# Hybrid decoder layer on one core: projection products moved ahead of the value products and transposes of each attention turn

## What is computed

```python
def reference(x, ...):                       # x: (1, 1024, 1024) float32
    xn = rms_norm(x, norm_mix_w[l])
    proj = xn @ w_in[l]                      # 6 parts of 512 columns: b, c, h, q, k, v
    ...
    yc = short_conv_mixer(c_b, c_c, c_h, conv_w[l])      # b * conv3(c * h)
    qh = rms_norm(to_heads(q), q_norm_w[l]).transpose(0, 2, 1, 3)     # 8 heads of 64
    kh = rms_norm(to_heads(k), k_norm_w[l]).transpose(0, 2, 1, 3)
    ya = stick_breaking_attention(qh, kh, vh).transpose(0, 2, 1, 3)
    ...
    x = x + jnp.concatenate([yc, ya], axis=-1) @ w_out[l]
    x = x + hierarchical_moe(rms_norm(x, norm_ffn_w[l]), ...)         # 32 experts, top 2

def stick_breaking_attention(q, k, v):       # in blocks of 128 queries, keys up to the block's end
        z = jnp.einsum('bhqd,bhkd->bhqk', qb, kb) * scale
        log_keep = jnp.where(mask, jax.nn.log_sigmoid(-z), 0.0)
        ...
        suffix = lax.cumsum(shifted, axis=3, reverse=True)
        A = jnp.where(mask, jnp.exp(jax.nn.log_sigmoid(z) + suffix), 0.0)
        outs.append(jnp.einsum('bhqk,bhkd->bhqd', A, vb).astype(v.dtype))
```

## Time and profile before

| | us |
|---|---|
| median of 3 runs | 1353.81 (1353.19 to 1359.11) |
| the profiled execution, its own time | 1361.15 |
| its span in the trace | 1359.5 |
| attention stage, about 115 to 565 of the span | 450 |
| PE busy in these 450 us | 416.47 |
| experts, about 750 to 1300 of the span | 550 |

### The profile page before, as it was taken

How to read it: one execution, slowest core, us unless ns; L and a number is a source line. 1 busy time by engine, 2 the same in 40 slices (tenths; PEclk the granted TensorE clock), 3 DMA queues, 4 the chain that set the end, 5 groups by cost and what they waited for, 6 DMA issues and landing times. The chain is left out here.

```text
span 1359.5 us, 16775 instructions
## 1 busy us (share of the span) xinstructions
PE 1218.1 (90%) x5870; PEld 984.5 (72%) x5870; DVE 871.8 (64%) x910; ACT 732.6 (54%) x918; POOL 146.9 (11%) x194
## 2 busy tenths in 40 slices
PE   6999989979998998799945999999999999999930
PEld 5887767757776776588834888888888888888830
DVE  4314434445335446533264999999999999999935
ACT  5332523453354244421104788888888888888820
POOL 1000000000000003010002011111111111111000
PEclk9999969988998998899956999999999999999975
DMA  7111100100100103331064899999999999999509
GB/s 205 33 31 32 32 16 16 32 15 1 32 16 16 32 16 124 140 155 47 32 263 149 317 375 384 389 386 381 380 386 381 380 383 385 378 386 388 206 17 370
DMA packets 57339, 261.89 MB, mean 193 GB/s; under 512 B 13008, under 2 KB 33488, under 8 KB 43984
## 3 DMA queue, kind: packets, MB, share of 16 engines
q1 hardware_dynamic: 46928, 240.31, 46.4%
q0 software_dynamic: 9216, 16.80, 3.3%
q10 hardware_dynamic: 1152, 4.19, 0.8%
HBM read 252.88 MB, written 25.17 MB: 205 GB/s over the span
## 5 line engine op out<-in xcount | busy, mean ns | idle before, releaser
L1246 DVE TENSOR_TENSOR e_lo<-W,e_hi 128x1024 fp32r<-128x1024 f32 x384 | 452.6, 1220 | 25.2 <-ACT e_hi L1240 22.3
L1240 ACT ACTIVATE e_hi<-W 128x1024 fp32r<-128x1024 f32 x384 | 403.4, 1060 | 96.4 <-PE ps L1211 94.5
L731 DVE TENSOR_TENSOR_SCAN kept<-kept 128x128 f32<-128x128 f32 (+7 forms) x64 | 91.0, 1422 | 228.6 <-ACT kept L588 191.7
L1209 PE MATMUL ps<-e_hi,xT_hi 128*128 128x512 f32 x512 | 204.2, 399 | 7.1 <-DVE e_lo L1246 7.1
L1211 PE MATMUL ps<-e_lo,xT_hi 128*128 128x512 f32 x512 | 201.3, 393 | 0.0
L1210 PE MATMUL ps<-e_hi,xT_lo 128*128 128x512 f32 x512 | 200.7, 392 | 0.0
L587 ACT ACTIVATE soft<-ps,q_scale 128x128 f32<-128x128 f32 (+7 forms) x54 | 38.1, 705 | 200.4 <-PE ps L456 189.2
L407 PE MATMUL ps<-xnT_hi,w_hi 128*128 128x512 f32 x320 | 128.9, 403 | 14.4 <-DVE u L699 6.9
L407 PE MATMUL ps<-xnT_lo,w_hi 128*128 128x512 f32 x320 | 128.5, 402 | 0.0
L407 PE MATMUL ps<-xnT_hi,w_lo 128*128 128x512 f32 x320 | 128.3, 401 | 0.0
L1209 PEld LDWEIGHTS ps<-e_hi,xT_hi 128*128 128x128 f32 x512 | 97.5, 190 | 26.9 <-issue 4.0
(11 more groups left out here) (211 smaller groups left out, 1845.8 us busy)
## 6 DMA issues: line engine op xcount, KB each, us to landing
W<-in_w_dram SPq DMA_DIRECT2D x96, 2048.0 KB, 10.7
w_raw<-in_w_in_dram SPq DMA_DIRECT2D x20, 512.0 KB, 4.0
yy<-y_rows SPq DMA_DIRECT2D x8, 1024.0 KB, 13.3
xt<-in_x_dram SPq DMA_DIRECT2D x8, 512.0 KB, 3.8
w_out_raw<-in_w_out_dram SPq DMA_DIRECT2D x4, 1024.0 KB, 8.0
xn_rows<-xn SPq DMA_DIRECT2D x8, 512.0 KB, 2.6
out_dram<-x ACTq DMA_DIRECT2D x8, 512.0 KB, 8.9
x<-in_x_dram SPq DMA_DIRECT2D x1, 3072.0 KB, 13.6
```

What stands on the lines that cost most here:

```text
L731: dve.tensor_tensor_scan(back, back, back, 1.0, ALU.mult, ALU.min).then_inc(multiplied, 1)
L1209: pe.matmul(o, xs_hi[:, k], e_hi[:, p, cols], start=(k == 0), stop=False)
L1240: act.activation(e_hi[:, p], flat[:, p * D:(p + 1) * D], ACT.Copy).then_inc(s["hi_made"], 1)
L1246: dve.tensor_tensor(e_lo[:, p], flat[:, p * D:(p + 1) * D], e_hi[:, p], ALU.subtract).then_inc(s["lo_made"], 1)
```

## The change

In a turn of PE the projection products are issued directly behind `scores(n + 1)`, ahead of `values(n - 2)` and `turn(n - 1)`, except in turns `JOIN[p]`, `JOIN[p] + 1` and `JOIN[p] + 2`, which keep the old order. In every turn of ScalarE the projection banks are emptied directly behind `open_unit(n + 1)`, ahead of `take_values` and `take_turned`. VectorE, GpSimd and SyncE keep their lists. No instruction is added or taken away.

```diff
--- before.py
+++ after.py
@@ -482,11 +482,15 @@
                     p, r = divmod(n, PU)
                     if r != JOIN[p] + 1 and n + 1 < UNITS:
                         scores(n + 1)
+                    early = r not in range(JOIN[p], JOIN[p] + 3)
+                    if early:
+                        project(ticks_by(n - 1), ticks_by(n))
                     if n >= 2:
                         values(n - 2)
                     if n:
                         turn(n - 1)
-                    project(ticks_by(n - 1), ticks_by(n))
+                    if not early:
+                        project(ticks_by(n - 1), ticks_by(n))
                     if r == JOIN[p] and p + 1 < NPAIR:
                         sums_of_qk(p + 1)
                     if r == JOIN[p] + 1:
@@ -633,12 +637,13 @@
                     p, r = divmod(n, PU)
                     if r != JOIN[p] + 1 and n + 1 < UNITS:
                         open_unit(n + 1)
+                    if n:
+                        for g in groups_in(n - 1):
+                            take(g)
                     if n >= 9 and n % 8 == 1:
                         take_values(n // 8 - 1)
                     if n:
                         take_turned(n - 1)
-                        for g in groups_in(n - 1):
-                            take(g)
```

## The result

| | before | changed |
|---|---|---|
| median, us | 1356.03 (4 runs, 1353.19 to 1359.11) | 1399.88 (4 runs, 1397.87 to 1402.61) |
| profiled execution, its own time | 1361.15 | 1401.07 |
| its span | 1359.5 | 1399.4 |

The changed kernel takes 1.0327 times as long, with a 95% interval of 1.0297 to 1.0358: 40 to 49 us more, 44 by the medians. The forecast was 33 more.

A forecast was written before the change was run, and what follows sets the result against it. PE's own work was taken to bound the attention stage, so every new hole adds: 18.0 us for scores plus 15.0 for projection banks, 33 on 1353.8, gives 1387 us; own range 1378 to 1396, 8 in 10 1367 to 1408.

The forecast's parts named there:

- Both mechanisms of the sum: PE's new waits in attention: for scores' second banks, 18.0 us, and for projection banks, 15.0 us.
- What bounds the stage: Attention stage: PE's own work sets an ordinary turn, busy 416.47 of 450 us; reordering can only fill or open holes.
- Part 1: Scores directly behind transposes: the second bank waits for the previous unit's opening in 17 turns, 18.0 us together.
- the formula: Wait per scores' second bank: opening less 0.51 us, from 0.75 in two pieces to 1.61 at 1024 columns.
- Part 2: Projections brought forward lose values and transposes as cover while their bank is emptied: waits of 15.0 us beyond Part 1.
- Part 3: ScalarE empties banks first: `probsT` comes one or two copies of 0.62 us later, covered by projections; taken as 0.
- The joins: Turns 9 to 11 keep their order and VectorE still empties behind weighing: holes stay, no delay won back.
- The second rival: New holes in attention also lower PE's clock, 19 us more: 1406 us, range 1396 to 1415; chance 0.20.
- Only part 1: Banks are emptied in time, so only the scores' waits of 18 us count: 1372 us, range 1366 to 1378; chance 0.18.
- nothing: PE's true slack per turn absorbs the waits, no measurable change: 1354 to 1360 us; chance 0.07.
- faster: Earlier projections fill banks sooner and shrink two holes at the joins by 5 us: 1344 us; chance 0.05.

The follow-up runs named there:

- the third buffer: A third `soft` buffer, added to the changed kernel: 1344.61 us, 0.9915 times the kernel before; added to the kernel before: 1340.29 us, 0.9878.
- the second profile: The kernel before, profiled again unchanged: span 1352.4 us; turns 11 to 13 of pair 0 took 20.4 us, against 26.1 in its first profile.

## Why the prediction was right, and where it was off

The measured 1399.88 us lie in the range of 8 in 10 (1367 to 1408) and outside the forecast's own range (1378 to 1396). Both mechanisms of the sum were found in their places; 10 of the 43 us were not in the sum.

- **What bounds the stage.** Right. PE has no holes in ordinary turns before, so a new hole is lost time, and its mark is in the distances between masks. What the step left out is that PE's own pace can change behind a hole.
- **Part 1, the scores' second bank: 18.0 us.** Right in place and count, and nearly in size. In two pieces the rows list 0.53, at 640 columns 0.74, at 768 0.95, at 896 1.15 to 1.17, at 1024 1.38 to 1.40. By the starts some 0.16 us more is lost each time (1.32 against 1.15 above): 0.69, 0.90, 1.11, 1.32 and 1.54, each 0.07 below the formula's 0.75, 0.97, 1.18, 1.39 and 1.61. All 17 are in the trace, with 14.1 us listed and 16.8 by the starts; the third buffer shows the cause.
- **Part 2, the projection banks: 15.0 us.** Right in place but for turn 6 of pairs 0 to 2, which has no wait (0.1 was forecast). VectorE's chain in turn 13 was forecast at 6.2 us from the end of the transposes; it is 208.31 - 202.2 = 6.1. But the waits there are shorter than the forecast 1.2 us, since PE came late to the bank at half clock: by the starts 0.3 us in pair 0 and 0.5 in pair 1. Turn 3 of pair 3 was forecast at 3.0 us from there; transposes end near 484.0 and the bank is used at 487.02. Turns 8 and 9 of pair 0 together take 3.1 us more than before (from the mask product of unit 8 to that of unit 10, 10.96 to 14.03); forecast were 3.0.
- **Part 3, ScalarE's order: 0.** Right as a sum: 1.0005 alone. Under PE's new order it saves some 5 us by the ratios, 1.0367 without it against 1.0327, with intervals that overlap.
- **The joins: nothing won back.** Not quite. Against the second profile the hole of pair 1's join shrank from 7.05 to 5.82 us and that of pair 2 from 2.24 to 1.49, and the stretches around them got 1.25 and 0.57 us shorter; pair 0's stayed at 5.9. The same joins gave 11 us once their cause in VectorE's list was taken away.
- **The step that failed is the sum's silence on the clock.** The second rival, with 0.20, put the loss of clock beside the forecast, and its 1396 to 1415 us hold the measured 1399.88. It came true in part, in six places and not in ten. From mask to mask, the turns with half clock took this much more than the forecast loss: in pair 3 3.0 us for turn 3 (4.9 lost instead of 1.9), 1.8 for turn 9 and 1.6 just before the join; 0.7 and 0.9 in turn 13 of pairs 0 and 1; and 1.6 in turn 14 of pair 1. Together 9.6 us; the second profile of the kernel before has full clock in all six. The sign that the prediction named for this rival, a clock of the stage well below 0.94, hardly showed: the mean over the stage is 0.93 in the changed kernel, 0.94 and 0.95 in the two profiles of the kernel before, since the stretches are short.
- **A term left out.** Turns without any wait got 0.05 to 0.06 us longer (from mask to mask 4.12 to 4.18, 4.23 to 4.28, 5.49 to 5.55 us). Over 50 turns that is some 3 us, which the 1.1 us saved in turn 2, the 1.8 at the joins and the 1.2 less of part 1 outweigh. The third buffer shows it apart from waits: up to unit 61 the changed order is 2.2 us behind the old one, though it saves 1.1 us in turn 2.
- **"Only part 1", "nothing" and "faster"** fell. Turn 2 of pair 0 shows what the third of these was about: a wait of PE for VectorE before the transposes (0.92 us) is covered now; it saves 1.1 us.

By the Trainium skill, Perfetto Trace Analysis, section Matmul Optimizations, matmuls should run back to back in batches because the engine adapts its power to utilization. The traces here agree in kind: clock 0.50 in the stretch behind the 1.89 us hole, 1.00 in the same stretch where a wait of 0.91 us was left of it. They don't say that each hole costs the clock: behind the wait of 0.84 us at 508.78 it stayed at 1.00.

## What to carry to other kernels

An order inside a loop is an order round the loop: moving the filler ahead of the values also took it from between transposes and scores, where it had hidden a chain through another engine. Before moving a filler, write down what it covers now: for each instruction behind it, what that waits for and when it is released. And where a wait goes back to a buffer's reuse, a further buffer may be worth more than any order; it was here, by 55 us in one order and 18 in the other.

## What the runs showed of the hardware

- A hole of 0.46 us in the midst of scores, value products and transposes was followed by half clock in one profile of the kernel before and not in the second one (mean clock 0.61 and 0.87 over the same 26 us): 5.7 us of difference from one execution to the next, in a kernel whose turns outside the joins are the same to 0.05 us in both. A profile's join is not to be taken as the kernel's without a second one.
- The same holds for a hole in an ordinary turn. The wait of 0.84 us in turn 6 of pair 3 was followed by full clock in the changed kernel (1.00 from 508 to 512) and by half clock in the kernel with projections forward only in short turns (0.62 from 484 to 488).
- The first score product starts 212.43 - 211.51 = 0.92 us after the start of seven transposes, where a projection product starts 207.50 - 206.76 = 0.74 after it. So what follows the transposes matters by 0.18 us. The reason stays open. The two rows in the changed kernel:

```profile
211.51 0.98 PE L456 MATMUL ps<-ident,soft 128*128 128x128 f32 x7
...
212.43 0.49 PE L443 MATMUL ps<-k_hi,q_hi 64*128 64x512 f32 x1
```
